# Renewal of semaphores ahead of a stage's last waits, gate products on another engine, and bias waits by class, in a two-layer diffusion trunk on one Trainium2 core

## The reference

```python
def trunk_layer(x, ctx, c, c_ctx, common, mixer, ctx_out):
    ...
    h = rmsnorm(x, g_pre_mix) * (1 + sc1) + sh1
    mix, mix_c = mixer(h, hc, ctx_out)
    x = x + gt1 * rmsnorm(mix, g_post_mix)
    h = rmsnorm(x, g_pre_ffn) * (1 + sc2) + sh2
    x = x + gt2 * rmsnorm(expert_choice_ffn(h, w_router, w_gate, w_up, w_down), g_post_ffn)
    if ctx_out:      # the same for ctx; only in layer 0
        ...
def differential_attention(q, k, v, lam):      # each head's output is then rmsnorm-ed
    p = softmax(einsum('bqhmd,bkhmd->bhmqk', q, k) * scale)
    return einsum('bhqk,bkhe->bqhe', p[:, :, 0] - lam * p[:, :, 1], v)
def expert_choice_ffn(h, w_router, w_gate, w_up, w_down):
    gate, idx = lax.top_k(swapaxes(softmax(h @ w_router), 1, 2), cap)     # 128 tokens, 32 of ctx
    hid = silu(xg @ w_gate) * (xg @ w_up)
    out = (hid @ w_down) * gate[..., None]
    return zeros_like(h).at[bidx, idx].add(out)
def ssd_output(y, xs, z, d_skip, gnorm_g):
    y = (y + d_skip * xs) * silu(z)
    y = y.reshape(b, L, D_GROUPS, D_INNER // D_GROUPS)
    return (y * rsqrt(mean(y * y) + eps)) * gnorm_g
```

## Time and profile before

| | |
|---|---|
| runs, median (lowest to highest) | 3753.34 us (3749.29 to 3756.32), 3 runs |
| the profiled execution | 3752.3 us, its span in the profile 3750.3 us |
| PE busy, share of the span | 3350.7 us, 89% |
| DVE, ACT, POOL busy | 1175.3, 956.2 and 509.9 us (31%, 25%, 14%) |
| stages, us from the span's start | attn_a 438 to 751.6; near to 992; mix0 to 1187; experts0 to 2127.4; front to 2371.9; scan to 2620.2; band, mix1 to 2951; experts1 to 3716.7; finish to 3750.3 |

### The profile page before, as it was taken

The page is one execution under the profiler, slowest core; times in us unless marked ns, Lnnn a source line. Parts: engine busy times, 40 slices in busy tenths (PEclk is TensorE's granted clock), DMA queues, the critical chain, the costliest instruction groups (busy, mean ns, idle before and its releaser), DMA issues. The chain is left out here.

```text
span 3750.3 us, 53356 instructions
## 1 busy us (share of the span) xinstructions
PE 3350.7 (89%) x20560; PEld 2492.0 (66%) x20560; DVE 1175.3 (31%) x2901; ACT 956.2 (25%) x2175; POOL 509.9 (14%) x660
## 2 busy tenths in 40 slices
PE   6999899879995799999999689897889399999995
PEld 4888655556552688778877555564665278888873
DVE  3222366556434210111011243565653511111102
ACT  3111266545321111111111132243542111111111
POOL 1010332200000001101110330244000000000002
PEclk8999999989997899999999889998999699999997
DMA  6336454452224687778777720101212579989896
GB/s 210 118 104 124 141 177 164 138 148 76 64 99 153 223 274 253 246 255 273 256 251 246 216 106 0 55 15 51 73 33 99 212 248 320 315 304 319 309 320 217
DMA packets 381875, 675.50 MB, mean 180 GB/s; under 512 B 80736, under 2 KB 119824, under 8 KB 375504
## 3 DMA queue, kind: packets, MB, share of 16 engines
q1 hardware_dynamic: 344608, 542.91, 42.5%
q10 hardware_dynamic: 23664, 83.90, 6.3%
q0 software_dynamic: 13456, 46.80, 5.1%
HBM read 587.38 MB, written 92.36 MB: 181 GB/s over the span
## 5 line engine op out<-in xcount | busy, mean ns | idle before, releaser
L2247 PE MATMUL experts_gu_ps<-experts_xT,experts_wg 128*128 128x160 f32 (+1 forms) x4096 | 551.9, 288 | 4.5 <-DVE experts_xT L2175 2.6
L2247 PE MATMUL experts_gu_ps<-experts_xT,experts_wu 128*128 128x160 f32 (+1 forms) x4096 | 549.7, 287 | 0.0
L2247 PEld LDWEIGHTS experts_gu_ps<-experts_xT,experts_wg 128*128 128x128 f32 x4096 | 529.0, 192 | 19.3 <-issue 19.3
L2247 PEld LDWEIGHTS experts_gu_ps<-experts_xT,experts_wu 128*128 128x128 f32 x4096 | 525.2, 191 | 0.0
L2217 PE MATMUL experts_y_ps<-experts_wd,experts_hid 128*128 128x512 f32 x1024 | 452.3, 597 | 0.0
L2188 DVE TENSOR_TENSOR experts_hid<-experts_sil,experts_gu_ps 128x160 f32<-128x160 f32 (+1 forms) x256 | 77.9, 304 | 941.4 <-ACT experts_sil L2152 941.4
L2152 ACT ACTIVATE experts_sil<-experts_gu_ps 128x160 f32<-128x160 f32 (+1 forms) x256 | 74.5, 291 | 1106.4 <-PE experts_gu_ps L2247 1106.4
L2217 PEld LDWEIGHTS experts_y_ps<-experts_wd,experts_hid 128*128 128x128 f32 x1024 | 190.6, 190 | 231.3 <-issue 228.5
L2116 POOL DMA_INDIRECT moe<-experts_y,experts_ixs x32 | 51.3, 1602 | 1130.5 <-DVE experts_y L2192 1130.5
L2192 DVE TENSOR_SCALAR experts_y<-experts_y_ps,experts_wt 128x512 f32<-128x512 f32 x32 | 24.0, 751 | 449.4 <-PE experts_y_ps L2217 449.4
L2547 PE MATMUL front_pb_ps<-kept_hT,front_ahead_w 128*128 128x512 f32 (+1 forms) x384 | 138.7, 521 | 0.7 <-DVE kept_dt L2599 0.7
(11 more groups left out here) (421 smaller groups left out, 4743.9 us busy)
## 6 DMA issues: line engine op xcount, KB each, us to landing
experts_wg<-in_l_w_gate SPq DMA_DIRECT2D x64, 2048.0 KB, 9.0
experts_wu<-in_l_w_up SPq DMA_DIRECT2D x64, 2048.0 KB, 12.9
experts_wd<-in_l_w_down SPq DMA_DIRECT2D x64, 2048.0 KB, 11.2
attn_a_mod_w<-in_l_w_mod ACTq DMA_DIRECT2D x36, 1024.0 KB, 4.8
proj<-proj_ob ACTq DMA_DIRECT2D x60, 256.0 KB, 2.3
proj_ahead_w<-in_l_w_in SPq DMA_DIRECT2D x6, 2048.0 KB, 9.6
mix_xr<-res SPq DMA_DIRECT2D x18, 512.0 KB, 4.0
res<-mix_xr ACTq DMA_DIRECT2D x18, 512.0 KB, 2.6
```

The source lines that it names most:

```text
L2247: mm = nc.tensor.matmul(GU[f % 2][:, part, 0:N], w[:, h, k, c * P:(c + 1) * P], xT[:, k, :], start=(k == 0), stop=(k == KD - 1))
```

## The change

- `st.renew(sp)` is called ahead of the last wait of SP in attn_a, experts and scan (there after the fifth store), and is dropped in finish.
- attn_a's last head is normalised in three calls: tiles 0 to 3, 4 to 7, 8 and 9.
- near's bias waits are by class: ten semaphores in place of two, waited for at the first tile of each class.
- mix, front and finish: the product with the gate no longer needs 1/rms. It is formed first (`tmp`, `mg`), and one operation then does `product * rs + x` (on the same engine, VectorE, as before in mix; in front the addition leaves GpSimd). In front GpSimd forms the products of tiles 1 to 9, in finish those of tiles 2, 4 and 6; VectorE the others. In front `memset(pad)` moves to a place behind tile 1.
- experts0: the scatter of `ctx` tokens is issued ahead of that of `x` tokens.
- scan: the rotation of the last tile is done by VectorE, between the last two `normed`.

The diff, cut to its core:

```diff
@@ attn_a, SP and GpSimd @@
+                st.renew(sp)
                 later.store(sp)
-                st.renew(sp)
...
-                normalise(H - 1, 0, NT - 2)
-                normalise(H - 1, NT - 2, NT)
+                ENDS = (0, 4, NT - 2, NT)
+                for first, end in zip(ENDS, ENDS[1:]):
+                    normalise(H - 1, first, end)
@@ near, VectorE @@
-                    if near and tile(n) == 0 and j == 0 and m == 0:
-                        dve.wait_ge(bias_in[pair % 2], START + 16 * len(PARTS) * (pair // 2 + 1))
+                    if near and tile(n) in (0, 1, 2, 6, 7) and j == 0 and m == 0:
+                        dve.wait_ge(bias_in[pair % 2][bias_class(tile(n))], START + 16 * 4 * (pair // 2 + 1))
@@ mix, VectorE, tail(n) @@
+                    dve.wait_ge(ms1, START + n + 1)
+                    nc.vector.tensor_tensor(tmp[:], Y[slot][:].rearrange("p a b -> p (a b)"), gate[:, cond, :], ALU.mult).then_inc(r_done, 1)
...
-                    nc.vector.tensor_tensor(xr[:, slot, :], tmp[:], xr[:, slot, :], ALU.add).then_inc(x_done, 1)
+                    nc.vector.scalar_tensor_tensor(xr[:, slot, :], tmp[:], rs[:, slot, 0:1], xr[:, slot, :], ALU.mult, ALU.add).then_inc(x_done, 1)
@@ experts, GpSimd, scatter(e) @@
+                    if with_ctx:
+                        pool.wait_ge(yc_out, START + e * YCS + YCS)
...
                     pool.wait_ge(yv, START + e + 1)
                     pool.wait_ge(ya, START + e + 1)
@@ finish, SP, GpSimd and VectorE @@
-                st.renew(sp)
...
+                def gated(t):
+                    pool.wait_ge(m_in[t], START + 16)
+                    nc.gpsimd.tensor_tensor(mg[:, t, :], m[:, t, :], gate[:], ALU.mult).then_inc(gated_done, 1)
...
                 for t in range(NTX):
+                    if t >= 2 and t % 2 == 0:
+                        gated(t)
                     rsqrt(t)
...
+                    if t >= 2 and t % 2 == 0:
+                        dve.wait_ge(gated_done, START + t // 2)
+                    else:
+                        dve.wait_ge(m_in[t], START + 16)
+                        nc.vector.tensor_tensor(mg[:, t, :], m[:, t, :], gate[:], ALU.mult).then_inc(m_done, 1)
...
+                    nc.vector.scalar_tensor_tensor(x[:, t, :], mg[:, t, :], ms[:, t:t + 1], x[:, t, :], ALU.mult, ALU.add).then_inc(x_done, 1)
@@ front, GpSimd and VectorE @@
                 for t in range(NT):
                     pool.wait_ge(msm_done, START + t + 1)
                     rsqrt(ms_moe[:, t:t + 1], rsm_done)
-                    if t >= 1:
-                        rstd_of(t - 1)
...
-                    nc.gpsimd.tensor_tensor(xt[:, s], mt[:, s], xt[:, s], ALU.add).then_inc(x_done, 1)
-                rstd_of(NT - 1)
+                    if t + 1 < NT:
+                        gated(t + 1)
+                    rstd_of(t)
+                    if t == 1:
+                        link(nc.gpsimd.memset(pad[:], 0.0))
...
-                    nc.vector.scalar_tensor_tensor(mt[:, s], mt[:, s], ms_moe[:, t:t + 1], gate[:, t // NTX, :], ALU.mult, ALU.mult).then_inc(m_done, 1)
+                    nc.vector.scalar_tensor_tensor(xt[:, s], mg[:, t % 2], ms_moe[:, t:t + 1], xt[:, s], ALU.mult, ALU.add).then_inc(x_done, 1)
@@ scan, SP and VectorE @@
+                    if j == 4:
+                        st.renew(sp)
...
+                dve.wait_ge(rotated, START + NTX - 1)
+                rotate(nc.vector, link, NTX - 1, rotated_last)
+                normed(NTX - 1)
```

More of the change, by code:

```diff
@@ L1254, in local_attention @@
             "ready s_done r_done rw_done t_done o_done o_out pool_step dve_step const_in").split())
-        q_in, k_in, v_in, bias_in = ([st.sem(f"{n}{s}") for s in range(2)] for n in ("q_in", "k_in", "v_in", "bias_in"))
+        q_in, k_in, v_in = ([st.sem(f"{n}{s}") for s in range(2)] for n in ("q_in", "k_in", "v_in"))
         rT_done = st.sem("rT_done")
@@ L1261, in local_attention @@
         if near:
+            bias_in = [[st.sem(f"bias_in{s}{cls}") for cls in range(CLASSES)] for s in range(2)]
             PARTS = [(h2, cls, a) for h2 in range(2) for cls in range(CLASSES) for a in range(2)]
@@ L2724, in rate, with rotate @@
             return v[:, t, d * H8:(d + 1) * H8]
+        def rotate(eng, link, t, done):
+            s = t % 2
+            pair = qk[:, s, :].rearrange("p (h n two) -> p h n two", two=2, n=HD)
+            c, si = (v[:, s, :].unsqueeze(1).to_broadcast([P, QK // 2 // HD, HD]) for v in (cos, sin))
+            part = [turn[:, i, :].rearrange("p (h n) -> p h n", n=HD) for i in range(4)]
+            link(eng.tensor_tensor(part[0], pair[:, :, :, 0], c, ALU.mult))
+            link(eng.tensor_tensor(part[1], pair[:, :, :, 1], si, ALU.mult))
+            link(eng.tensor_tensor(part[2], pair[:, :, :, 0], si, ALU.mult))
+            link(eng.tensor_tensor(part[3], pair[:, :, :, 1], c, ALU.mult))
+            link(eng.tensor_tensor(pair[:, :, :, 0], part[0], part[1], ALU.subtract))
+            eng.tensor_tensor(pair[:, :, :, 1], part[2], part[3], ALU.add).then_inc(done, 1)
         with nc.Block() as block:
@@ L2834, in store_q @@
                 def store_q(t):
-                    act.wait_ge(rotated, START + t + 1)
+                    if t < NTX - 1:
+                        act.wait_ge(rotated, START + t + 1)
+                    else:
+                        act.wait_ge(rotated_last, START + 1)
                     act.dma_start(proj[t * P:(t + 1) * P, 0:QK], qk[:, t % 2, :]).then_inc(q_out[t % 2], 16)
```

88 lines of the change are left out of this document (43 added, 45 removed).

## The result

The changed kernel takes 3720.98 us (median of 4 runs, 3718.38 to 3722.08) against 3751.58 before (4 runs, 3749.29 to 3756.32): a ratio of 0.9915 with a 95% interval of 0.9903 to 0.9927, so 30.6 us or 0.8% less. The forecast was 3727, within 3712 to 3738.

The account below looks back on a forecast made before the run. TensorE is busy nearly all the time in the experts stages, unchanged; gains lie at stage ends, starts and three tile loops. Terms sum to -26.3 us, taking the profiled 3752.3 to 3726.0, median 3727, range 3712 to 3738.

Parts of the forecast that it names:

- attn_a: End of attn_a: split normalisation lets GpSimd end at 748.8 and SP at 748.4, -2.7 us (bounds 0 and -3.0).
- near: Start of near: waiting for bias by class removes nearly all of VectorE's 8.66 us idle time, -8.3 us.
- scan, resets: End of scan: last norm 3.0 us earlier with the rotation on VectorE, resets -4.4, together -7.4 us.
- I take the drain as tied to the last scatter: Experts stages' ends: GpSimd's drain ends 7.7 us after its last scatter began; experts0 -3.1 us, experts1 -2.6.
- finish: Finish: GpSimd's products and VectorE exclude each other, 7.6 us a pair against 5.0; with resets gone, +1.6 us.
- front: Front's tile loop: 7.1 us a tile against 7.42, memset +1.2, in sum -2.0 us (bounds -6 and +3).
- My own sign of error: The forecast counts as wrong if front's squares come under 6.8 us apart; others were finish under 30 us, experts0's clock not 0.96.
- Rival A: Finish and front: GpSimd and VectorE run beside each other, finish -8, front -6, sum -39.9, 3713.5 us; chance 0.12.
- C: Finish and front: the products cost more, +3 us each, sum -19.9, 3733.5 us; chance 0.16.
- B: Near's bias wait only moves, -4 us, and experts' ends give -4; sum -20.3, 3733 us; chance 0.16.
- D: Stage ends: resets do not hide; attn_a 0, experts -4, scan -4, sum -18.5, 3735 us; chance 0.06.
- E: Experts stages: TensorE's granted clock 2% lower costs 34 us more, the result slower than before; chance 0.04.

Follow-up runs that it names:

- Experiment 3: The kernel before with only the places of the semaphore resets changed (none in finish): 3740.03 us, ratio 0.9970.
- experiment 4: The kernel before with only near's bias waits made by class: 3744.22 us, ratio 0.9978; near 234.9 us.
- experiment 7: The changed kernel with scan's last rotation back on GpSimd: 3724.3 us, ratio 0.9927; scan 244.1 us.
- experiments 1: The changed kernel with all eight of finish's gate products on VectorE: 3718.09 us, ratio 0.9905; finish 27.6 us.
- 10: The changed kernel with front's gate products on VectorE and the memset first again, finish as in the changed kernel: 3716.46 us, ratio 0.9906.
- 11: The changed kernel with all gate products of finish and front on VectorE and the memset first again, a repeat: 3714.03 us, ratio 0.9901.
- experiment 9: The changed kernel run once more, unchanged: 3721.38 us, ratio 0.9918; front 235.3 us.

## Why the prediction was right, and where it was not

**attn_a.** The step was right, -2.6 for -2.7. These rows answer to the earlier trace rows:

```profile
746.07 0.19 POOL L814 TENSOR_SCALAR attn_a_ms<-attn_a_ms 128x2 f32<-128x2 f32 x1 [0.17 <-ACT attn_a_sq L865]
```

and by line the drains of TensorE's and GpSimd's queues, whose ends are the start plus the duration in ns:

```profile
L769 PEldq DRAIN  x1: 1700/1700/1700, 744.6 to 744.6; - x1
...
L769 POOLq DRAIN  x1: 558/558/558, 751.4 to 751.4; - x1
```

GpSimd's last call begins at 746.07, right after ScalarE's last tile, and not 2.7 us after it; from TensorE's last work to the end it is 5.8 us in every kernel with this part, 8.4 in every one without. Experiment 3 has only the resets and stays at 8.4: it is the split that does it. The stage was no shorter in the shown pair because its middle took 308.2 us and not 305.3. The forecast had no term for that, and it is not the change's: the middle took 305.3 to 308.5 us in four profiles without the split and 305.2 to 308.9 in nine with it. Two rows of the changed kernel, 115 us into the stage:

```profile
552.76 2.91 POOL L817 TENSOR_TENSOR attn_a_ob<-attn_a_ob,attn_a_ahead_g 128x1280 f32<-128x1280 f32 x1
...
553.22 3.79 DVE L932 SCALAR_TENSOR_TENSOR attn_a_a<-attn_a_e,attn_a_c 128x1280 f32<-128x1280 f32 x1
```

and the same place in the second profile of the changed kernel:

```profile
550.48 1.55 DVE L932 SCALAR_TENSOR_TENSOR attn_a_a<-attn_a_e,attn_a_c 128x1280 f32<-128x1280 f32 x1
...
550.84 3.38 POOL L816 TENSOR_TENSOR attn_a_ob<-attn_a_ob,attn_a_ms 128x1280 f32<-128x1280 f32 x1
```

Where GpSimd's product starts first, VectorE's map takes 3.79 us; where VectorE is first, it takes 1.55 and GpSimd's product 3.38. This is the rule of the Trainium skill ("SBUF — State Buffer", "Who interferes with whom"), that the order of issue decides who blocks, with 2.2 us for VectorE or 1.0 for GpSimd here. Ten or eleven maps over 1.7 us went with a middle of 308.1 to 308.9 us (four profiles), nine with 305.2 to 307.4 (nine), in kernels old and new; no run forces the one or the other, so it is argued and not shown that the collision makes the 3 us. (Of the slow maps of the earlier trace rows eight stood beside GpSimd's rotations, but the longest, 3781 ns, beside a product like the one above.)

**near.** The term was 1.0 too large. The bias wait went as forecast (8.47 of 8.66); what the sum lacked was that matmuls then ran at the lower clock for 3.6 us longer. In the shown pair VectorE's maxima are 8.5 us ahead of those before over the first two tiles and 7.0 after the next one, in which the kernel before has its clock back and the changed one has not; the lead is 7.3 at the end. The size of this hangs on the execution, as experiment 4 shows.

**scan, resets.** -7.4 for -7.4, and in finish and scan 4.3 us for the resets as computed. The rotation is worth 3.1 of the 3.0 forecast (experiment 7).

**mix.** The stages gave -1.4 for -1.8, but that is not all. mix1 and the loop of experts1 together took 914.3 to 914.4 us in the four profiles with the old form and 912.1 to 912.4 in the nine with the new one, some 2.1 less. In the shown pair 0.5 of it lies in mix1 and 1.6 in experts1, where the stretch at the lower clock with which the stage begins ended 60.2 us after its start and not 62.8; in experiments 1, 10 and 11 mix1 itself was 1.9 us shorter and the loop 753.7 to 753.8 us as before. Only mix's form is both new in all nine and next to these stages; no run has it alone.

**experts.** experts1's end gave -2.8 for -2.6; the rest of its 4.3 is the part of mix's gain just told, for which the forecast had no term. In experts0 the step "I take the drain as tied to the last scatter" failed: it is tied to the landing. The end gave -1.8 (12.6 to 10.8 us), 0.8 to 1.4 by the resets and 1.0 by the order, for -3.1.

**finish.** The mechanism was right, the size off. The two exclude each other, and VectorE ends later; but by 2.8 us, not 6.2. The pair takes 6.48 and not 7.6. I had counted both a turn of 0.5 us that GpSimd's power waits for and 1/rms of 0.85; in the trace the power for tile 3 (1.56 us from 3699.29 on) runs beside VectorE's sum and product and costs nothing of its own. The other 0.6 are small: GpSimd's product ends 2.2 us after VectorE's (3701.58 to 3703.78) and not 2.35, the sum beside it ends 1.08 after that and not 1.28, 1/rms takes 0.78, and the handovers nothing. With two such pairs, a start 0.5 us earlier and an end 0.5 us shorter the forecast was 3.3 us too long. Net -1.4 for +1.6.

**front.** The exclusion came as forecast, two sizes did not. One is the new chain, "7.1" a tile. Where the product comes first, a tile takes 6.74: from a square to the next product are 3.27 us, as added up, but the sum ends 1.09 us after the product and not 1.28, and the handover of 0.2 is not there. The last tile, with no product beside its sum, takes 5.23. With the memset (8.07 us at its tile, so +1.3 for +1.2) the way from the first square to the last is 60.5 us, where my numbers give 65.1: that is 4.6 of the 6.4 us by which the shown pair was off. The other is "squares started at 2136.8 and 2203.6, 7.42 a tile", taken as the form's own pace. It is a mean of 6.82 and of tiles in which VectorE waited for slow matmuls; the four other profiles of the old form have 6.80 to 7.01 in the mean. In that profile the part behind the last square took 168.2 us, where the four others have 166.5, and that was another 1.7 us of the 6.4.

The two errors worked against each other. With the usual 6.95 a tile for before, my sum would have come to about +2, where the four calm profiles of the old form (238.4 us in the mean) and the five of the new (235.7) differ by -2.7; with the outlier of 244.5 among the old ones it is -3.9. That the forecast had the right sign here was luck. The pace of 6.74 is hardly under 6.82, and the memset costs 1.3: what is gained is that VectorE's wait for the keys no longer adds to the tiles (the squares keep their 6.74 us beside matmuls of 5.25 us), and the last tile. My own sign of error, squares under 6.8 apart, showed it.

So -26.3 became -31.4 in the profiles: front 6.4, finish 3.0 and experts1 1.7 more than forecast, attn_a 3.0, experts0 1.2 and near 1.0 less, mix 0.4 less. That the time came within 6 us of 3727 is in part luck, since errors of 11 us on the one side and 6 on the other nearly met; the mechanisms behind near, scan, the resets and the split are shown by their own runs. Rival A (products hidden) is refuted by the rows of 3.3 us; C did not come; B and D came in small parts; E did not: the granted clock in experts0 was 0.96 again.

## What to carry to other kernels

Before moving an elementwise product from VectorE to GpSimd, ask whether VectorE has instructions with two inputs from SBUF in the same stretch: then the move costs the length of GpSimd's instruction (2.35 us here for VectorE's 1.22), and pays only if it takes a wait out of a chain. At a stage's end, list the end of each engine's queue, the drains too, and count a change only down to the next one. And take a stage's pace from the shortest repeat in the trace, with the waits apart: a mean over one execution may hold the clock of that execution, as front's 7.42 did. Two profiles of the same program show which stages differ by themselves.

## What the runs showed of the hardware

- VectorE and GpSimd took turns whole instructions long: the sum took 1.28 us alone, 3.32 in front beside a product of 2.35 us on GpSimd that had started 0.12 us earlier, and 3.25 in finish.
- Who was first decided who waited: where VectorE's sum came ahead of GpSimd's product (front, tile 8 of experiment 9), the sum took 1.28 us and the product 2.88.
- The drain of GpSimd's queue after indirect transfers lasted until 1.4 us (experts1) or 2.75 us (experts0) after the last landing, in each of the thirteen profiles. Why the two differ is open.
- TensorE's granted clock in near went to 1.00 6.3 us after the first maximum in the kernel before and 9.9 us after it in the changed one, and a seventh of the wait that was won (1.2 of 8.47 us) was lost there; the repeat of the same program had the rise 5.6 us earlier in the stage and near 1.8 us shorter.
- attn_a's middle, 305 to 309 us, differed by up to 3.7 us between executions, as much as most of the single edits here. The longer ones had one or two more collisions of VectorE's map with an instruction of GpSimd.
